# Exchanging the places of two groups of tensors in SBUF: a stage-tensor region and the weight rings

## Fill

filler text here. filler text here. filler text here. filler text here. filler text here. filler text here. filler text here. filler text here. filler text here. filler text here. filler text here. filler text here. filler text here. filler text here. filler text here. filler text here. filler text here. filler text here. filler text here. filler text here. filler text here. filler text here. filler text here. filler text here. filler text here. filler text here. filler text here. filler text here. filler text here. filler text here. filler text here. filler text here. filler text here. filler text here. filler text here. filler text here. filler text here. filler text here. filler text here. filler text here. filler text here. filler text here. filler text here. filler text here. filler text here. filler text here. filler text here. filler text here. filler text here. filler text here. filler text here. filler text here. filler text here. filler text here. filler text here. filler text here. filler text here. filler text here. filler text here. filler text here. filler text here. filler text here. filler text here. filler text here. filler text here. filler text here. filler text here. filler text here. filler text here. filler text here. filler text here. filler text here. filler text here. filler text here. filler text here. filler text here. filler text here. filler text here. filler text here. filler text here. filler text here. filler text here. filler text here. filler text here. filler text here. filler text here. filler text here. filler text here. filler text here. filler text here. filler text here. filler text here. filler text here. filler text here. filler text here. filler text here. filler text here. filler text here. filler text here. filler text here. filler text here. filler text here. filler text here. filler text here. filler text here. filler text here. filler text here. filler text here. filler text here. filler text here. filler text here. filler text here. filler text here. filler text here. filler text here. filler text here. filler text here. filler text here. filler text here. filler text here. filler text here. filler text here. filler text here. filler text here. filler text here. filler text here. filler text here. filler text here. filler text here. filler text here. filler text here. filler text here. filler text here. filler text here. filler text here. filler text here. filler text here. filler text here. filler text here. filler text here. filler text here. filler text here. filler text here. filler text here. filler text here. filler text here. filler text here. filler text here. filler text here. filler text here. filler text here. filler text here. filler text here. filler text here. filler text here. filler text here. filler text here. filler text here. filler text here. filler text here. filler text here. filler text here. filler text here. filler text here. filler text here. filler text here. filler text here. filler text here. filler text here. filler text here. filler text here. filler text here. filler text here. filler text here. filler text here. filler text here. filler text here. filler text here. filler text here. filler text here. filler text here. filler text here. filler text here. filler text here. filler text here. filler text here. filler text here. filler text here. filler text here. filler text here. filler text here. filler text here. filler text here. filler text here. filler text here. filler text here. filler text here. filler text here. filler text here. filler text here. filler text here. filler text here. filler text here. filler text here. filler text here. filler text here. filler text here. filler text here. filler text here. filler text here. filler text here. filler text here. filler text here. filler text here. filler text here. filler text here. filler text here. filler text here. filler text here. filler text here. filler text here. filler text here. filler text here. filler text here. filler text here. filler text here. filler text here. filler text here. filler text here. filler text here. filler text here. filler text here. filler text here. filler text here. filler text here. filler text here. filler text here. filler text here. filler text here. filler text here. filler text here. filler text here. filler text here. filler text here. filler text here. filler text here. filler text here. filler text here. filler text here. filler text here. filler text here. filler text here. filler text here. filler text here. filler text here. filler text here. filler text here. filler text here. filler text here. filler text here. filler text here. filler text here. filler text here. filler text here. filler text here. filler text here. filler text here. filler text here. filler text here. filler text here. filler text here. filler text here. filler text here. filler text here. filler text here. filler text here. filler text here. filler text here. filler text here. filler text here. filler text here. filler text here. filler text here. filler text here. filler text here. filler text here. filler text here. filler text here. filler text here. filler text here. filler text here. filler text here. filler text here. filler text here. filler text here. filler text here. filler text here. filler text here. filler text here. filler text here. filler text here. filler text here. filler text here. filler text here. filler text here. filler text here. filler text here. filler text here. filler text here. filler text here. filler text here. filler text here. filler text here. filler text here. filler text here. filler text here. filler text here. filler text here. filler text here. filler text here. filler text here. filler text here. filler text here. filler text here. filler text here. filler text here. filler text here. filler text here. filler text here. filler text here. filler text here. filler text here. filler text here. filler text here. filler text here. filler text here. filler text here. filler text here. filler text here. filler text here. filler text here. filler text here. filler text here. filler text here. filler text here. filler text here. filler text here. filler text here. filler text here. filler text here. filler text here. filler text here. filler text here. filler text here. filler text here. filler text here. filler text here. filler text here. filler text here. filler text here. filler text here. filler text here. filler text here. filler text here. filler text here. filler text here. filler text here. filler text here. filler text here. filler text here. filler text here. filler text here. filler text here. filler text here. filler text here. filler text here. filler text here. filler text here. filler text here. filler text here. filler text here. filler text here. filler text here. filler text here. filler text here. filler text here. filler text here. filler text here. filler text here. filler text here. filler text here. filler text here. filler text here. filler text here. filler text here. filler text here. filler text here. filler text here. filler text here. filler text here. filler text here. filler text here. filler text here. filler text here. filler text here. filler text here. filler text here. filler text here. filler text here. filler text here. filler text here. filler text here. filler text here. filler text here. filler text here. filler text here. filler text here. filler text here. filler text here. filler text here. filler text here. filler text here. filler text here. filler text here. filler text here. filler text here. filler text here. filler text here. filler text here. filler text here. filler text here. filler text here. filler text here. filler text here. filler text here. filler text here. filler text here. filler text here. filler text here. filler text here. filler text here. filler text here. filler text here. filler text here. filler text here. filler text here. filler text here. filler text here. filler text here. filler text here. filler text here. filler text here. filler text here. filler text here. filler text here. filler text here. filler text here. filler text here. filler text here. filler text here. filler text here. filler text here. filler text here. filler text here. filler text here. filler text here. filler text here. filler text here. filler text here. filler text here. filler text here. filler text here. filler text here. filler text here. filler text here. filler text here. filler text here. filler text here. filler text here. filler text here. filler text here. filler text here. filler text here. filler text here. filler text here. filler text here. filler text here. filler text here. filler text here. filler text here. filler text here. filler text here. filler text here. filler text here. filler text here. filler text here. filler text here. filler text here. filler text here. filler text here. filler text here. filler text here. filler text here. filler text here. filler text here. filler text here. filler text here. filler text here. filler text here. filler text here. filler text here. filler text here. filler text here. filler text here. filler text here. filler text here. filler text here. filler text here. filler text here. filler text here. filler text here. filler text here. filler text here. filler text here. filler text here. filler text here. filler text here. filler text here. filler text here. filler text here. filler text here. filler text here. filler text here. filler text here. filler text here. filler text here. filler text here. filler text here. filler text here. filler text here. filler text here. filler text here. filler text here. filler text here. filler text here. filler text here. filler text here. filler text here. filler text here. filler text here. filler text here. filler text here. filler text here. filler text here. filler text here. filler text here. filler text here. filler text here. filler text here. filler text here. filler text here. filler text here. filler text here. filler text here. filler text here. filler text here. filler text here. filler text here. filler text here. filler text here. filler text here. filler text here. filler text here. filler text here. filler text here. filler text here. filler text here. filler text here. filler text here. filler text here. filler text here. filler text here. filler text here. filler text here. filler text here. filler text here. filler text here. filler text here. filler text here. filler text here. filler text here. filler text here. filler text here. filler text here. filler text here. filler text here. filler text here. filler text here. filler text here. filler text here. filler text here. filler text here. filler text here. filler text here. filler text here. filler text here. filler text here. filler text here. filler text here. filler text here. filler text here. filler text here. filler text here. filler text here. filler text here. filler text here. filler text here. filler text here. filler text here. filler text here. filler text here. filler text here. filler text here. filler text here. filler text here. filler text here. filler text here. filler text here. filler text here. filler text here. filler text here. filler text here. filler text here. filler text here. filler text here. filler text here. filler text here. filler text here. filler text here. filler text here. filler text here. filler text here. filler text here. filler text here. filler text here. filler text here. filler text here. filler text here. filler text here. filler text here. filler text here. filler text here. filler text here. filler text here. filler text here. filler text here. filler text here. filler text here. filler text here. filler text here. filler text here. filler text here. filler text here. filler text here. filler text here. filler text here. filler text here. filler text here. filler text here. filler text here. filler text here. filler text here. filler text here. filler text here. filler text here. filler text here. filler text here. filler text here. filler text here. filler text here. filler text here. filler text here. filler text here. filler text here. filler text here. filler text here. filler text here. filler text here. filler text here. filler text here. filler text here. filler text here. filler text here. filler text here. filler text here. filler text here. filler text here. filler text here. filler text here. filler text here. filler text here. filler text here. filler text here. filler text here. filler text here. filler text here. filler text here. filler text here. filler text here. filler text here. filler text here. filler text here. filler text here. filler text here. filler text here. filler text here. filler text here. filler text here. filler text here. filler text here. filler text here. filler text here. filler text here. filler text here. filler text here. filler text here. filler text here. filler text here. filler text here. filler text here. filler text here. filler text here. filler text here. filler text here. filler text here. filler text here. filler text here. filler text here. filler text here. filler text here. filler text here. filler text here. filler text here. filler text here. filler text here. filler text here. filler text here. filler text here. filler text here. filler text here. filler text here. filler text here. filler text here. filler text here. filler text here. filler text here. filler text here. filler text here. filler text here. filler text here. filler text here. filler text here. filler text here. filler text here. filler text here. filler text here. filler text here. filler text here. filler text here. filler text here. filler text here. filler text here. filler text here. filler text here. filler text here. filler text here. filler text here. filler text here. filler text here. filler text here. filler text here. filler text here. filler text here. filler text here. filler text here. filler text here. filler text here. filler text here. filler text here. filler text here. filler text here. filler text here. filler text here. filler text here. filler text here. filler text here. filler text here. filler text here. filler text here. filler text here. filler text here. filler text here. filler text here. filler text here. filler text here. filler text here. filler text here. filler text here. filler text here. filler text here. filler text here. filler text here. filler text here. filler text here. filler text here. filler text here. filler text here. filler text here. filler text here. filler text here. filler text here. filler text here. filler text here. filler text here. filler text here. filler text here. filler text here. filler text here. filler text here. filler text here. filler text here. filler text here. filler text here. filler text here. filler text here. filler text here. filler text here. filler text here. filler text here. filler text here. filler text here. filler text here. filler text here. filler text here. filler text here. filler text here. filler text here. filler text here. filler text here. filler text here. filler text here. filler text here. filler text here. filler text here. filler text here. filler text here. filler text here. filler text here. filler text here. filler text here. filler text here. filler text here. filler text here. filler text here. filler text here. filler text here. filler text here. filler text here. filler text here. filler text here. filler text here. filler text here. filler text here. filler text here. filler text here. filler text here. filler text here. filler text here. filler text here. filler text here. filler text here. filler text here. filler text here. filler text here. filler text here. filler text here. filler text here. filler text here. filler text here. filler text here. filler text here. filler text here. filler text here. filler text here. filler text here. filler text here. filler text here. filler text here. filler text here. filler text here. filler text here. filler text here. filler text here. filler text here. filler text here. filler text here. filler text here. filler text here. filler text here. filler text here. filler text here. filler text here. filler text here. filler text here. filler text here. filler text here. filler text here. filler text here. filler text here. filler text here. filler text here. filler text here. filler text here. filler text here. filler text here. filler text here. filler text here. filler text here. filler text here. filler text here. filler text here. filler text here. filler text here. filler text here. filler text here. filler text here. filler text here. filler text here. filler text here. filler text here. filler text here. filler text here. filler text here. filler text here. filler text here. filler text here. filler text here. filler text here. filler text here. filler text here. filler text here. filler text here. filler text here. filler text here. filler text here. filler text here. filler text here. filler text here. filler text here. filler text here. filler text here. filler text here. filler text here. filler text here. filler text here. filler text here. filler text here. filler text here. filler text here. filler text here. filler text here. filler text here. filler text here. filler text here. filler text here. filler text here. filler text here. filler text here. filler text here. filler text here. filler text here. filler text here. filler text here. filler text here. filler text here. filler text here. filler text here. filler text here. filler text here. filler text here. filler text here. filler text here. filler text here. filler text here. filler text here. filler text here. filler text here. filler text here. filler text here. filler text here. filler text here. filler text here. filler text here. filler text here. filler text here. filler text here. filler text here. filler text here. filler text here. filler text here. filler text here. filler text here. filler text here. filler text here. filler text here. filler text here. filler text here. filler text here. filler text here. filler text here. filler text here. filler text here. filler text here. filler text here. filler text here. filler text here. filler text here. filler text here. filler text here. filler text here. filler text here. filler text here. filler text here. filler text here. filler text here. filler text here. filler text here. filler text here. filler text here. filler text here. filler text here. filler text here. filler text here. filler text here. filler text here. filler text here. filler text here. filler text here. filler text here. filler text here. filler text here. filler text here. filler text here. filler text here. filler text here. filler text here. filler text here. filler text here. filler text here. filler text here. filler text here. filler text here. filler text here. filler text here. filler text here. filler text here. filler text here. filler text here. filler text here. filler text here. filler text here. filler text here. filler text here. filler text here. filler text here. filler text here. filler text here. filler text here. filler text here. filler text here. filler text here. filler text here. filler text here. filler text here. filler text here. filler text here. filler text here. filler text here. filler text here. filler text here. filler text here. filler text here. filler text here. filler text here. filler text here. filler text here. filler text here. filler text here. filler text here. filler text here. filler text here. filler text here. filler text here. filler text here. filler text here. filler text here. filler text here. filler text here. filler text here. filler text here. filler text here. filler text here. filler text here. filler text here. filler text here. filler text here. filler text here. filler text here. filler text here. filler text here. filler text here. filler text here. filler text here. filler text here. filler text here. filler text here. filler text here. filler text here. filler text here. filler text here. filler text here. filler text here. filler text here. filler text here. filler text here. filler text here. filler text here. filler text here. filler text here. filler text here. filler text here. filler text here. filler text here. filler text here. filler text here. filler text here. filler text here. filler text here. filler text here. filler text here. filler text here. filler text here. filler text here. filler text here. filler text here. filler text here. filler text here. filler text here. filler text here. filler text here. filler text here. filler text here. filler text here. filler text here. filler text here. filler text here. filler text here. filler text here. filler text here. filler text here. filler text here. filler text here. filler text here. filler text here. filler text here. filler text here. filler text here. filler text here. filler text here. filler text here. filler text here. filler text here. filler text here. filler text here. filler text here. filler text here. filler text here. filler text here. filler text here. filler text here. filler text here. filler text here. filler text here. filler text here. filler text here. filler text here. filler text here. filler text here. filler text here. filler text here. filler text here. filler text here. filler text here. filler text here. filler text here. filler text here. filler text here. filler text here. filler text here. filler text here. filler text here. filler text here. filler text here. filler text here. filler text here. filler text here. filler text here. filler text here. filler text here. filler text here. filler text here. filler text here. filler text here. filler text here. filler text here. filler text here. filler text here. filler text here. filler text here. filler text here. filler text here. filler text here. filler text here. filler text here. filler text here. filler text here. filler text here. filler text here. filler text here. filler text here. filler text here. filler text here. filler text here. filler text here. filler text here. filler text here. filler text here. filler text here. filler text here. filler text here. filler text here. filler text here. filler text here. filler text here. filler text here. filler text here. filler text here. filler text here. filler text here. filler text here. filler text here. filler text here. filler text here. filler text here. filler text here. filler text here. filler text here. filler text here. filler text here. filler text here. filler text here. filler text here. filler text here. filler text here. filler text here. filler text here. filler text here. filler text here. filler text here. filler text here. filler text here. filler text here. filler text here. filler text here. filler text here. filler text here. filler text here. filler text here. filler text here. filler text here. filler text here. filler text here. filler text here. filler text here. filler text here. filler text here. filler text here. filler text here. filler text here. filler text here. filler text here. filler text here. filler text here. filler text here. filler text here. filler text here. filler text here. filler text here. filler text here. filler text here. filler text here. filler text here. filler text here. filler text here. filler text here. filler text here. filler text here. filler text here. filler text here. filler text here. filler text here. filler text here. filler text here. filler text here. filler text here. filler text here. filler text here. filler text here. filler text here. filler text here. filler text here. filler text here. filler text here. filler text here. filler text here. filler text here. filler text here. filler text here. filler text here. filler text here. filler text here. filler text here. filler text here. filler text here. filler text here. filler text here. filler text here. filler text here. filler text here. filler text here. filler text here. filler text here. filler text here. filler text here. filler text here. filler text here. filler text here. filler text here. filler text here. filler text here. filler text here. filler text here. filler text here. filler text here. filler text here. filler text here. filler text here. filler text here. filler text here. filler text here. filler text here. filler text here. filler text here. filler text here. filler text here. filler text here. filler text here. filler text here. filler text here. filler text here. filler text here. filler text here. filler text here. filler text here. filler text here. filler text here. filler text here. filler text here. filler text here. filler text here. filler text here. filler text here. filler text here. filler text here. filler text here. filler text here. filler text here. filler text here. filler text here. filler text here. filler text here. filler text here. filler text here. filler text here. filler text here. filler text here. filler text here. filler text here. filler text here. filler text here. filler text here. filler text here. filler text here. filler text here. filler text here. filler text here. filler text here. filler text here. filler text here. filler text here. filler text here. filler text here. filler text here. filler text here. filler text here. filler text here. filler text here. filler text here. filler text here. filler text here. filler text here. filler text here. filler text here. filler text here. filler text here. filler text here. filler text here. filler text here. filler text here. filler text here. filler text here. filler text here. filler text here. filler text here. filler text here. filler text here. filler text here. filler text here. filler text here. filler text here. filler text here. filler text here. filler text here. filler text here. filler text here. filler text here. filler text here. filler text here. filler text here. filler text here. filler text here. filler text here. filler text here. filler text here. filler text here. filler text here. filler text here. filler text here. filler text here. filler text here. filler text here. filler text here. filler text here. filler text here. filler text here. filler text here. filler text here. filler text here. filler text here. filler text here. filler text here. filler text here. filler text here. filler text here. filler text here. filler text here. filler text here. filler text here. filler text here. filler text here. filler text here. filler text here. filler text here. filler text here. filler text here. filler text here. filler text here. filler text here. filler text here. filler text here. 

## The chip, the cores and the metric

The kernel runs on one core of one Trainium2 chip. The metric is the device time of one execution in microseconds (us); a median over several executions is compared.

## What is computed

The reference chains two small transformer blocks, each with two layers, over 256 tokens of width 1024, in float32.

```python
def reference(x, c, ctx, c_ctx, w_ada, ..., w_gate_2, w_up_2, w_down_2):
    x = first_block(x, c, ctx, c_ctx, w_ada, ...)      # 2 layers
    return second_block(x, attn_norm_g_2, w_in_2, ...) # 2 layers
```

A layer of the first block takes a modulation from the condition vectors (`silu(cond) @ w_ada`, 1024 x 6144), normalizes and modulates the latent and the context stream (256 tokens each), multiplies by `w_in` (1024 x 1536), mixes by attention, a Fourier transform and a gated spatial product, multiplies by `w_out` (1024 x 1024), and runs a squared-ReLU MLP of width 4096. In its second layer the context stream ends early. A layer of the second block multiplies the 256 latent tokens by `w_in_2` (1024 x 3656), runs three kinds of attention, multiplies by `w_out_2`, and runs a gated MLP of width 2816.

## The kernel before

The float32 products with weights are made of three products of a reduced format (`float32r`): a weight slot `raw` is split into a high part `w_hi` (ScalarE, `split`, L1101) and a rest `w_lo = raw - w_hi` (VectorE, `split`, L1467), an activation likewise into a high part and a rest, and `three` (L2049) issues three matmuls into the same PSUM tile: high by high, high by low and low by high. Of a matmul's two operands, one is loaded into TensorE (the stationary one, 128 columns, shown as LDWEIGHTS), the other streams through it (the moving one, 256, 328 or 512 columns). Which is which depends on the stage:

| stage (time in the profile) | moving | stationary | columns |
|---|---|---|---|
| `rows1`, `down("out1")` of the first block (30 to 113, 200 to 247, 620 to 675, 720 to 750) | ring of weights | `act_hi`, `act_lo` | 512 |
| `up1`, first block's MLP in, layer 0 (247 to 345, 443 to 522) | `act_hi`, `act_lo` | ring of weights | 512 |
| `up1`, layer 1 (750 to 850) | `act_hi`, `act_lo` | ring of weights | 256 |
| `down("mlp1")`, MLP out (345 to 435, 522 to 607, 850 to 939) | ring of weights | `hid1_hi`, `hid1_lo` | 512 |
| `rows2`, `down("out2")` of the second block (940 to 1090, 1284 to 1433) | ring of weights | `act_hi`, `act_lo` | 512, 328, 256 |
| `up2` (1095 to 1221, 1437 to 1564) | `act_hi`, `act_lo` | ring of weights | 256 |
| `down("mlp2")` (1221 to 1283, 1564 to 1625) | ring of weights | `hid2_hi`, `hid2_lo` | 512 |

The rings are `raw` and `w_lo` with 8 slots and `w_hi` with 5, each slot 1024 floats (4,096 bytes) per partition. In the second block `w_hi` has a sixth slot, in a tensor of its own, `w_hi2` (`hi_of`): of each six consecutive slots of weights one has its high part there. In the profile's names buffer numbers are left out, so `w_hi2` reads `w_hi`, `hid1_hi` and `hid2_hi` read `hid_hi`. The slots are filled by DMAs from SyncE's queue in the fixed order of the program (`put`, L804); 40 slots of `w_lo` are stored to HBM and fetched back later (`split_lo`).

The modulation (`ada`, L2118) multiplies plain float32 out of `raw` by `cond` in 32-column tiles. Every wait is a semaphore; the order of the work on each engine is written out by hand in tables (`FILL`, `FILL2`, `OUT2`).

SBUF is laid out by hand as well. `sb` hands out tensors one behind the other in the order of the calls, each start rounded up to 32 bytes, and what is entered in an `ExitStack` gives its bytes back when the `with` ends, so that what is allocated next lies on the same bytes. So `raw` and `w_lo` share one place (`w_lo` overwrites a slot of `raw` as it is computed), and the tensors of the two blocks' stages share one region:

```python
        with ExitStack() as s:
            raw = sb("raw", [P, RAW, 1024], F32, s)
        w_lo = sb("w_lo", [P, RAW, 1024], F32R)
        w_hi = sb("w_hi", [P, SPLIT, 1024], F32R)
```

## Time and profile before

| | |
|---|---|
| median of 3 runs | 1634.4 us (1633.2 to 1635.25) |
| the profiled execution's own time | 1630.14 us |
| its span | 1628.3 us |
| granted TensorE clock, mean | 0.995 |
| TensorE matmuls (PE) | 1571.9 us busy, 97% of the span |
| weight loads (PEld) | 1280.5 us, 79% |
| VectorE (DVE) | 1029.1 us, 63% |
| ScalarE (ACT) | 793.5 us, 49% |
| GpSimd (POOL) | 115.2 us, 7% |
| moved by DMA | 322.41 MB, mean 198 GB/s |

Busy time is the time in which at least one instruction of the engine is in flight. Matmuls overlap each other, so their mean duration is longer than the distance from one start to the next; the distance (the pitch) is what a stream of matmuls costs. In the chain of waits a piece "PE ... x48" gives it: its time divided by its count.

### The profile page before, as it was taken

How to read it: one execution, taken by the hardware profiler on the slowest of the kernel's cores; microseconds unless marked ns; L12 is line 12 of the kernel's file. 1: busy time of each engine (PE TensorE's matmuls, PEld its weight loads, DVE VectorE, ACT ScalarE, POOL GpSimd, SP SyncE). 2: the span in 40 equal slices, each digit the busy share in tenths (PEclk: the TensorE clock that was granted, in tenths of full speed). 3: DMA queues.
4: the chain of work that ended last, by engine and by line, in shares of the span. 5: the costliest groups of instructions: out<-in, count | busy, mean ns of one | idle time of the engine just before them, and what ended most of it. 6: DMA issues, size and time to landing. Idle time of an engine off the chain costs nothing.

```text
span 1628.3 us, 23404 instructions
## 1 busy us (share of the span) xinstructions
PE 1571.9 (97%) x9126; PEld 1280.5 (79%) x9126; DVE 1029.1 (63%) x1585; ACT 793.5 (49%) x1346; POOL 115.2 (7%) x130
## 2 busy tenths in 40 slices
PE   6999999999999998998999999999999999999999
PEld 2864776788888887567998878779998787799987
DVE  3637654663356327576775476878885558878863
ACT  3536623551246225564664456655454456555442
POOL 0211000000000001100000030100000101000000
PEclk8999999999999999999999999999999999999999
DMA  9438533882367433576998699336665696356653
GB/s 358 143 115 295 199 97 123 279 282 93 108 232 275 149 91 100 186 263 193 336 322 269 195 302 307 119 117 182 184 188 185 197 318 205 96 146 187 186 183 114
DMA packets 201005, 322.41 MB, mean 198 GB/s; under 512 B 14576, under 2 KB 100864, under 8 KB 200768
## 3 DMA queue, kind: packets, MB, share of 16 engines
q1 hardware_dynamic: 192992, 293.51, 56.0%
q0 software_dynamic: 7680, 27.34, 4.6%
q8 instruction: 73, 1.20, 0.3%
q14 instruction: 36, 0.29, 0.1%
q10 hardware_dynamic: 224, 0.07, 0.0%
HBM read 298.27 MB, written 22.61 MB: 197 GB/s over the span
## 4 chain that ended last, share of the span: by engine, by line
PE 89%; DVE 5%; DMA 3%; ACT 2%; issue 1%; POOL 1%; SPq 0%; POOLq 0%; DVEq 0%; ACTq 0%
PE bank L2049 54%; PE pair_bank L2049 21%; PE bank L2118 2%; PE pair_bank L2309 1%; PE bank L2340 1%; PE bank L2320 1%; PE pair_bank L2360 1%; PE bank L2582 1%; PE bank L2250 1%; DVE w_lo L1467 1%; DMA raw<-in_w_in 1%; PE bank L2144 1%; DMA raw<-in_w_ada 1%; PE bank L2230 1%; DMA raw<-in_w_mlp 1%
## 5 line engine op out<-in xcount | busy, mean ns | idle before, releaser
L1467 DVE TENSOR_TENSOR w_lo<-raw,w_hi 128x1024 fp32r<-128x1024 f32 (+1 forms) x374 | 447.9, 1219 | 283.7 <-ACT w_hi L1101 281.8
L1101 ACT CAST w_hi<-raw 128x1024 fp32r<-128x1024 f32 (+2 forms) x416 | 427.7, 1044 | 389.6 <-PE bank L2049 285.8
L2049 PE MATMUL pair_bank<-act_hi,w_hi 128*128 128x256 f32 (+1 forms) x736 | 230.4, 313 | 8.7 <-DVE act_lo L1545 3.4
L2049 PE MATMUL pair_bank<-act_hi,w_lo 128*128 128x256 f32 (+1 forms) x736 | 227.0, 308 | 0.0
L2049 PE MATMUL pair_bank<-act_lo,w_hi 128*128 128x256 f32 (+1 forms) x736 | 226.9, 308 | 0.0
L2049 PE MATMUL bank<-w_hi,hid_lo 128*128 128x512 f32 x560 | 221.3, 395 | 0.0
L2049 PE MATMUL bank<-w_hi,hid_hi 128*128 128x512 f32 x560 | 221.3, 395 | 0.0
L2049 PE MATMUL bank<-w_lo,hid_hi 128*128 128x512 f32 x560 | 221.3, 395 | 0.0
L2049 PE MATMUL bank<-w_hi,act_hi 128*128 128x512 f32 (+2 forms) x528 | 205.9, 390 | 6.5 <-DVE act_lo L1578 2.1
L2049 PE MATMUL bank<-w_hi,act_lo 128*128 128x512 f32 (+2 forms) x528 | 199.2, 377 | 0.0
L2049 PE MATMUL bank<-w_lo,act_hi 128*128 128x512 f32 (+2 forms) x528 | 198.9, 377 | 0.0
L2049 PEld LDWEIGHTS pair_bank<-act_hi,w_hi 128*128 128x128 f32 x736 | 140.2, 190 | 23.5 <-DVE act_lo L1545 5.7
L2049 PEld LDWEIGHTS pair_bank<-act_lo,w_hi 128*128 128x128 f32 x736 | 140.2, 191 | 7.4 <-issue 1.0
L2049 PEld LDWEIGHTS pair_bank<-act_hi,w_lo 128*128 128x128 f32 x736 | 140.2, 191 | 6.9
L2049 PE MATMUL bank<-act_hi,w_hi 128*128 128x256 f32 (+1 forms) x480 | 145.0, 302 | 0.6 <-DVE w_lo L1467 0.6
L2049 PE MATMUL bank<-act_hi,w_lo 128*128 128x256 f32 (+1 forms) x480 | 144.3, 301 | 0.0
L2049 PE MATMUL bank<-act_lo,w_hi 128*128 128x256 f32 (+1 forms) x480 | 144.3, 301 | 0.0
L2049 PEld LDWEIGHTS bank<-w_hi,hid_lo 128*128 128x128 f32 x560 | 105.1, 188 | 25.5
L2049 PEld LDWEIGHTS bank<-w_lo,hid_hi 128*128 128x128 f32 x560 | 105.1, 188 | 25.3
L2049 PEld LDWEIGHTS bank<-w_hi,hid_hi 128*128 128x128 f32 x560 | 105.2, 188 | 25.2
L2049 PEld LDWEIGHTS bank<-w_hi,act_hi 128*128 128x128 f32 x528 | 99.7, 189 | 27.7 <-issue 4.2
L2049 PEld LDWEIGHTS bank<-w_hi,act_lo 128*128 128x128 f32 x528 | 99.5, 188 | 18.7
(238 smaller groups left out, 2102.3 us busy)
## 6 DMA issues: line engine op xcount, KB each, us to landing
raw<-in_w_mlp SPq DMA_DIRECT2D x128, 512.0 KB, 4.4
raw<-in_w_in SPq DMA_DIRECT2D x112, 512.0 KB, 4.5
raw<-in_w_ada SPq DMA_DIRECT2D x96, 512.0 KB, 5.7
raw<-in_w_gate SPq DMA_DIRECT2D x44, 512.0 KB, 3.8
raw<-in_w_up SPq DMA_DIRECT2D x44, 512.0 KB, 3.8
raw<-in_w_down SPq DMA_DIRECT2D x44, 512.0 KB, 3.5
split_lo<-w_lo POOLq DMA_DIRECT2D x36, 512.0 KB, 4.9
w_lo<-split_lo SPq DMA_DIRECT2D x36, 512.0 KB, 5.1
```

The lines of the kernel that those rows point to most:

```text
L1101: nc.scalar.copy(hi_of(i)[:, 0:w], raw[:, i % RAW, 0:w]).then_inc(hi_ready, 1)
L1467: nc.vector.tensor_tensor(w_lo[:, i % RAW, 0:w], raw[:, i % RAW, 0:w], hi_of(i)[:, 0:w].bitcast(F32), ALU.subtract).then_inc(lo_ready, 1)
L2049: ins = nc.tensor.matmul(o, a[x], b[y], start=first and i == 0, stop=True, skip_group_check=True)
L2118: ins = nc.tensor.matmul(bank[bk][j:j + 32, :], cond[:, k, :], tiles(raw[:, r, :], 2)[:, kk, :], start=k < 4, stop=True, skip_group_check= ...
L2144: nc.tensor.matmul(bank[bk][:], sel_b[:, s, :], mod_rows[:, bk % 2, :], start=True, stop=True, skip_group_check=True).then_inc(ada_turned, 1)
L2230: ins = nc.tensor.transpose(bank[b][:, i * P:(i + 1) * P], x, ident)
L2250: ins = nc.tensor.matmul(bank[5][:], proj1[:, 2 * s + t, F1 + i * P:F1 + (i + 1) * P], dft_n[:, t, :], start=t == 0, stop=t == TT - 1)
L2309: nc.tensor.matmul(bank[a][:, 0:w], st["q"][a], st["k"][a], start=True, stop=True).then_inc(scored, 1)
L2320: ins = nc.tensor.matmul(st["o"][a], st["v"][a][kt], probs_t1[:, j % 2, a, kt, :], start=kt == 0, stop=kt == keys - 1)
L2340: ins = nc.tensor.transpose(bank[2 + a][:, kt * P:(kt + 1) * P], probs1[:, j % 2, a, kt * P:(kt + 1) * P], ident)
L2360: nc.tensor.matmul(bank[a][:, 0:w], st["q"][a], st["k"][a], start=True, stop=False)
L2582: ins = nc.tensor.matmul(bank[2][:, (h - h0) * wd:(h - h0 + 1) * wd], pair("iq", h, t * P, t * P + P), pairs_t[half:half + DH, PAIR["ik"], ...
```

## Rows read from the trace of the kernel before

**Rows 1.** The page: busy us (share) and count; busy tenths and granted clock.
```profile
PE 1571.9 (97%) x9126; PEld 1280.5 (79%) x9126; DVE 1029.1 (63%) x1585; ACT 793.5 (49%) x1346; POOL 115.2 (7%) x130
...
PE   6999999999999998998999999999999999999999
...
PEclk8999999999999999999999999999999999999999
```

**Rows 2.** Chain of waits: shares of the span.
```profile
PE 89%; DVE 5%; DMA 3%; ACT 2%; issue 1%; POOL 1%; SPq 0%; POOLq 0%; DVEq 0%; ACTq 0%
```

**Rows 3.** Costliest groups by shape: count, busy us, mean ns, idle before.
```profile
L1467 DVE TENSOR_TENSOR w_lo<-raw,w_hi 128x1024 fp32r<-128x1024 f32 x368 | 441.7, 1222 | 276.5 <-ACT w_hi L1101 274.6
L1101 ACT CAST w_hi<-raw 128x1024 fp32r<-128x1024 f32 x404 | 417.0, 1047 | 369.4 <-PE bank L2049 283.3 <-PE pair_bank L2049 62.7 <-DMA raw<-in_w_mlp 13.3
L2049 PE MATMUL bank<-w_hi,hid_lo 128*128 128x512 f32 x560 | 221.3, 395 | 0.0
...
L2049 PE MATMUL bank<-w_hi,act_hi 128*128 128x512 f32 x448 | 181.0, 404 | 5.7 <-DVE act_lo L1578 2.1 <-DVE w_lo L1467 1.9 <-DMA w_lo<-split_lo 1.2
...
L2049 PE MATMUL pair_bank<-act_hi,w_hi 128*128 128x256 f32 x560 | 160.1, 286 | 6.8 <-DVE act_lo L1545 2.5 <-DVE w_lo L1467 2.1 <-DVE act_lo L1578 2.1
...
L2049 PE MATMUL bank<-act_hi,w_lo 128*128 128x256 f32 x400 | 113.2, 283 | 0.0
...
L2049 PE MATMUL pair_bank<-act_hi,w_hi 128*128 128x512 f32 x176 | 70.3, 399 | 2.0 <-DVE act_lo L1545 0.8 <-DVE w_lo L1467 0.6 <-ACT fa L1372 0.5
...
L2118 PE MATMUL bank<-raw,cond 128*32 128x512 f32 x384 | 51.8, 623 | 6.2 <-DMA raw<-in_w_ada 5.2 <-DVE cond L1477 1.1
```

**Rows 4.** Chain of waits, first 60 us: start us, us, what.
```profile
4.52 11.47 DMA raw<-in_w_ada
...
45.60 14.54 PE bank L2049 x64
```

**Rows 5.** Chain of waits, whole span, its longest pieces.
```profile
345.20 89.59 PE bank L2049 x384
...
500.07 10.88 PE pair_bank L2049 x48
...
826.64 11.52 PE pair_bank L2049 x96
...
951.35 8.75 DMA w_lo<-split_lo
...
1118.12 11.47 PE pair_bank L2049 x96
...
1221.48 61.47 PE bank L2049 x264
...
1300.20 7.98 DMA raw<-in_w_in
```

**Rows 6.** Single matmuls of rows2 in order: start us, us, engine, line.
```profile
973.74 0.39 PE L2049 MATMUL bank<-w_hi,act_hi 128*128 128x512 f32 x1
...
975.10 0.39 PE L2049 MATMUL bank<-w_hi,act_hi 128*128 128x512 f32 x1
...
977.67 0.40 PE L2049 MATMUL bank<-w_hi,act_lo 128*128 128x512 f32 x1
```

**Rows 7.** The same, single matmuls of up2.
```profile
1141.17 0.28 PE L2049 MATMUL pair_bank<-act_hi,w_lo 128*128 128x256 f32 x1
...
1143.77 0.28 PE L2049 MATMUL pair_bank<-act_hi,w_hi 128*128 128x256 f32 x1
...
1145.93 0.28 PE L2049 MATMUL pair_bank<-act_hi,w_hi 128*128 128x256 f32 x1
```

**Rows 8.** Busy us of each engine by stretch; granted clock, DMA share, GB/s.
```profile
10.00:40.00 30.00, 20.86 (x106) 10.29 (x103) 12.17 (x37) 13.81 (x34) 1.98 (x2) 0.83 1.03 384
...
939.00:1095.00 156.00, 147.85 (x829) 115.76 (x828) 115.49 (x269) 91.47 (x211) 27.07 (x24) 1.00 0.65 214
1095.00:1221.00 126.00, 126.00 (x1054) 126.00 (x1055) 109.05 (x88) 62.55 (x77) 0.00 (x0) 1.00 0.62 181
```

56 lines of the change are left out of this document (29 added, 27 removed).

## Prediction

> **What bounds the kernel now.** I read the page first, then the chain of waits, then the groups by shape, and then single matmuls. TensorE is busy for 97% of the span, nine tenths or more in 37 of the 40 slices, at full clock behind the first slice [rows 1]. The chain that ended last runs through it for 89% of the span; VectorE has 5% of it, DMA 3%, ScalarE 2% [rows 2]. So the price of this change is, above all, what it does to the pitch of TensorE's matmuls, and, next, to the waits for transfers. The instructions are the same before and after; what differs is the byte at which each operand lies.
>
> The trace shows that such a thing can matter. Four stages run long stretches without any idle time, so their pitch can be read from the chain [rows 5]. Where both operands are rings or `act` tensors, 48 matmuls of 512 columns take 10.88 us, 226.7 ns each; the same with the roles exchanged gives 14.54 us for 64, 227.2 ns [rows 4]. Where the stationary operand is `hid1`, 384 matmuls of the same shape take 89.59 us, 233.3 ns, 6.6 ns more. With `hid2` it is 61.47 us for 264, 232.8 ns. The duration column does not show this well (395 ns against 404, since it has waits in it) [rows 3]; the pitch does. With 256 columns and both operands in rings and `act`, 96 take 11.52 us, 120.0 ns. None of these stretches waits for anything, so the difference lies in the operands, and all that differs is where they lie. By the table of starts, rings and `act` tensors start at a multiple of 128 bytes; `hid1` starts 32 bytes behind one and `hid2` 96 bytes behind one.
>
> A third case is in the trace: `w_hi2`, which starts 64 bytes behind a multiple of 128. As the moving operand in `rows2` it has 11 pitches from 975.10 to 977.67 us, 233.6 ns each, right behind six of an ordinary ring slot from 973.74 to 975.10, 226.7 ns [rows 6]. As the stationary operand in `up2` it goes the other way: 22 pitches from 1141.17 to 1143.77 us, 118.2 ns, then 18 of the next slot to 1145.93, 120.0 ns [rows 7].
>
> **The change part by part.** The plain reading of these rows is that the pitch hangs on the remainder of the starts within 128 bytes. I take it as the rule for the sum and price each tensor by it.
>
> 1. Rings, `const`, `act`. All keep remainder 0. Price 0: 226.7 and 120.0 ns stay. This is the term with the greatest weight, since 3 x 448 and 3 x 176 matmuls of 512 columns and 3 x (560 + 400) of 256 columns hang on it [rows 3]. The nearest rows bound it: upwards 6.6 ns more per 512-column matmul (as `hid1`), which is 1,872 x 6.6 ns = 12.4 us; downwards 1.8 ns less per 256-column matmul (as `w_hi2`), about 2,530 x 1.8 ns = 4.6 us when the sixth that `w_hi2` has already is left out. I take 0, since among the starts seen those with remainder 0 agree wherever in their tensors they lie.
>
> 2. `hid1` goes from remainder 32 to 96, `hid2` from 96 to 32. Both remainders are in the trace, at 233.3 and 232.8 ns, and the second has one slot in six with `w_hi2` in it. Exchanging them costs 0; the lost `w_hi2` mixture costs 0.5 ns x 2 x 264 = +0.3 us. Full relief of both would be 3 x 560 x 6.6 ns = -11.1 us [rows 3], and it needs a remainder 0, which they don't get.
>
> 3. `w_hi2` goes from remainder 64 to 0. In `up2` its slots lose their advantage. The two stretches have 1,054 and as many matmuls [rows 8], a sixth of them is 350, by 1.8 ns = +0.6 us; the chain's pieces of 96 say about the same, 11.47 us here against 11.52 in `up1`, which has no `w_hi2` [rows 5]. In `rows2` and `down("out2")` it gains: 12 slots by the ring's count, 12 matmuls each, by 6.9 ns = -1.0 us. But these slots are where TensorE waits between slots (147.85 us busy in 156) [rows 8], so part of it only lengthens a wait. I take half, -0.5 us, with 0 and -1.0 as ends.
>
> 4. `cond` goes from remainder 0 to 64 as the stationary operand of the modulation (L2118, 384 rows for 192 matmuls, 623 ns) [rows 3]. With 7 ns either way it is 1.3 us at most. I take 0, because much of that work stands in the first 40 us behind its transfers [rows 4].
>
> 5. VectorE and ScalarE. The split takes 1222 ns and the cast 1047 ns for 1024 elements [rows 3]; both work on the rings, whose remainder by 128 stays. I take 0. If it were 1% on both, the cover is their idle time (276.5 and 369.4 us ahead of these two groups), save in the starts of stages where the chain goes through them.
>
> 6. Transfers. Nothing changes in number, size, order or queue. I take 0; the bound is in the rivals.
>
> Sum: +0.3 + 0.6 - 0.5 = +0.4 us. The profiled execution took 1630.14 us, so it would be 1630.5; the median of the runs is 1634.4, 4.3 us above it, and the forecast on that scale is 1634.8 us. A measurement of this kernel can tell about 0.2%, 3.3 us, from no change, so this is no change.
>
> The Trainium skill ("SBUF — State Buffer", specifications and the section on the bandwidth-pool intuition) says that lines of SBUF are 16 bytes and that TensorE has two read ports of its own, independent for moving and stationary operands. By that, starts at multiples of 32 bytes would all cost the same and the sum would be 0.0. The trace does not agree: 233.3 against 226.7 ns.
>
> **The rivals.**
>
> *Slower: the offset between rings and `act` counts beyond 128 bytes.* Before, rings and `act` tensors all start at 128 by the remainder of 256; now the rings start at 0 and `act` stays at 128. No steady stretch before has two operands that differ by just 128, so the trace cannot exclude that this costs what 32 bytes cost in `hid1`. It decides in the stages `rows1`, `down("out1")`, `up1`, `rows2`: if it hits both roles, +12.4 us, 1647.2; if only the rings as stationary operand (528 matmuls), +3.5 us, 1638.3. For it: a difference of 64 in `w_hi2` did change the pitch, by +6.9 ns when moving. Against: nothing in the trace varies with a larger remainder.
>
> *Faster: the same offset helps.* As with `w_hi2` in `up2`, the 256-column matmuls fall from 120.0 to 118.2 ns: -4.6 us, and the +0.6 of step 3 is not lost: 1629.6.
>
> *Faster: it is not the remainder but the half of SBUF.* `hid1`, `hid2` and `w_hi2` all lie above byte 131,072 before, the rings and `act` below it. If `hid` is slow for that reason, it now gets 226.7 ns for most of its parts: -11.1 us, 1623.7, and 1627.2 if the rings as stationary operand pay the same price in 528 matmuls. For it: the `w_hi2` rows fit neither reading well. Against: there `w_hi2` above the line is faster, not slower, with 256 columns.
>
> *Faster by transfers.* From 10 to 40 us the DMA engines are busy throughout (share 1.03, 384 GB/s) [rows 8] and the chain waits 11.47 us for them [rows 4]; later waits are 8.75 and 7.98 us [rows 5]. If a packet into `raw` gets cheaper by 128 of its 2,048 bytes, 6% of 30 us is -1.9 us, 1632.9, which is within no change. The Trainium skill ("DMA: Bandwidth & Descriptors", how a descriptor splits into AXI transactions) says that a transaction must start at a multiple of 256 bytes and that what lies before an unaligned start is fetched for nothing. The slots of `raw` start at remainder 128 before and 0 now, and by that rule this is the case that comes true. No row here shows it.
>
> That the change does not do what it says can be put aside: the starts in the built program are the new ones, and `hole` adds no instruction.
>
> **How the numbers follow.** Forecast 0.56, transfers 0.05, faster by the offset 0.12, faster by the half 0.08, slower in one role 0.07, slower in both 0.12. Within 0.2% are the first two, 0.61; faster 0.20; slower 0.19. The range takes in the forecast, the transfers, the gain by the offset and the loss in one role; left out are the loss in both roles and the half of SBUF, 0.20. With the ends of steps 3 and 4 it is 1628 to 1640 us.
>
> **What the profile after would show.** Right: 226.7 ns for 512 columns in `up1` (10.88 us for 48), 233.3 ns with `hid1` and `hid2` (89.6 us for 384, 61.6 for 264), 120.0 ns for every piece of `up2` (11.52, no 11.47), 226.7 ns for the sixth slot in `rows2`. Wrong: a pitch other than 226.7 or 120.0 ns in any of the long stretches with rings and `act` (the offset), 226.7 ns in the stretch from 345 us (the half), or a first chain piece for `raw<-in_w_ada` shorter than 11 us with the clock and matmuls unchanged (the transfers).

## The result, and the change that it belongs to

The part ahead of the prediction went on record with a mistake of mine: right behind the title it holds a block of filler words that says nothing, and its section on the change is missing, with the table of starts that the prediction reads. That section stands here instead. It is not part of what was recorded; its table follows from the calls of `sb` in the two kernels.

### The change

The calls of `sb` are put in another order. Before: `residual`, `act_hi`, `act_lo`, then `raw`/`w_lo`, `w_hi`, `const` and the small tensors, then the stages' tensors. Now the stages' tensors come directly behind `act_lo`; a tensor `hole` of 24,352 floats (97,408 bytes) per partition, which nothing reads or writes, is allocated when they have been given back, so that it covers just their region; and `raw`/`w_lo`, `w_hi`, `const` and the small tensors lie behind it.

```diff
+HOLE = 24352
...
         act_lo = sb("act_lo", [P, KT, 2 * NT], F32R)
-        with ExitStack() as s:
-            raw = sb("raw", [P, RAW, 1024], F32, s)
-        w_lo = sb("w_lo", [P, RAW, 1024], F32R)
-        w_hi = sb("w_hi", [P, SPLIT, 1024], F32R)
-        const = sb("const", [P, sum(CONSTS.values())])
...
-        lam = sb("lam", [P, DEPTH, 8])
-        g_rows = residual
-
         with ExitStack() as s:
             cond_raw = sb("cond_raw", [P, KT, 2], F32, s)
...
             with ExitStack() as s2:
                 xn2 = sb("xn2", [P, TT, D], F32, s2)
+        hole = sb("hole", [P, HOLE])
+        with ExitStack() as s:
+            raw = sb("raw", [P, RAW, 1024], F32, s)
+        w_lo = sb("w_lo", [P, RAW, 1024], F32R)
+        w_hi = sb("w_hi", [P, SPLIT, 1024], F32R)
+        const = sb("const", [P, sum(CONSTS.values())])
...
+        lam = sb("lam", [P, DEPTH, 8])
+        g_rows = residual
```

No instruction is added, removed, moved or given another shape: the diff touches calls of `sb` alone, and the two traces have the same count of instructions on every engine. Only the bytes differ at which operands lie. These are the starts in bytes within a partition, with the remainder by 128 and by 256:

| tensor | before | mod 128 | mod 256 | after | mod 128 | mod 256 |
|---|---|---|---|---|---|---|
| `residual` | 16512 | 0 | 128 | 16512 | 0 | 128 |
| `act_hi` | 32896 | 0 | 128 | 32896 | 0 | 128 |
| `act_lo` | 49280 | 0 | 128 | 49280 | 0 | 128 |
| `raw`, `w_lo` | 65664 | 0 | 128 | 163072 | 0 | 0 |
| `w_hi` | 98432 | 0 | 128 | 195840 | 0 | 0 |
| `const` | 118912 | 0 | 128 | 216320 | 0 | 0 |
| `cond` | 131712 | 0 | 128 | 65728 | 64 | 192 |
| `w_hi2` | 134720 | 64 | 64 | 68736 | 0 | 128 |
| `hid1_hi` | 155296 | 32 | 160 | 89312 | 96 | 224 |
| `hid1_lo` | 188064 | 32 | 160 | 122080 | 96 | 224 |
| `hid2_hi` | 138848 | 96 | 96 | 72864 | 32 | 160 |
| `hid2_lo` | 161376 | 96 | 96 | 95392 | 32 | 160 |
| `proj1` | 155296 | 32 | 160 | 89312 | 96 | 224 |

All stage tensors move down by 65,984 bytes, the rings and constants up by 97,408 bytes. Parts of a tensor begin at multiples of 512 bytes from its start in the large products, save the 328-column slots of `rows2`, which begin at multiples of 1,312 bytes.

### The times

| | before | after |
|---|---|---|
| median of 5 runs | 1634.4 us (1633.2 to 1635.25) | 1642.83 us (1636.96 to 1644.41) |
| the profiled execution | 1630.14 us, span 1628.3 | 1643.58 us, span 1641.8 |
| granted TensorE clock, mean | 0.995 | 0.988 |

The ratio is 1.0041, with an interval of 1.0029 to 1.0052. By the medians the kernel is slower by 8.4 us, by the ratio by 6.7 us (4.7 to 8.5). The forecast was no change, 1634.8, and the time lies outside the range of 1628 to 1640. The median of before is over five runs here; the part ahead had three of them, with the same median.

The page of the kernel after: busy us and counts, the granted clock in 40 slices, and the shares of the chain (beside [rows 1, 2]).

```profile
PE 1588.1 (97%) x9126; PEld 1285.7 (78%) x9126; DVE 1029.3 (63%) x1585; ACT 793.8 (48%) x1346; POOL 115.2 (7%) x130
...
PEclk8999999999999999999999999999999999999999
...
PE 90%; DVE 4%; DMA 2%; ACT 2%; issue 1%; POOL 1%; SPq 0%; POOLq 0%; DVEq 0%; ACTq 0%
```

TensorE is busy 16.2 us longer with the same 9,126 matmuls, and the chain's shares are those of before to within a point. So it is the pitch, not a new wait. The groups by shape (count, busy us, mean ns, idle before), beside [rows 3]:

```profile
L1469 DVE TENSOR_TENSOR w_lo<-raw,w_hi 128x1024 fp32r<-128x1024 f32 x368 | 441.5, 1221 | 279.8 <-ACT w_hi L1103 278.2
L1103 ACT CAST w_hi<-raw 128x1024 fp32r<-128x1024 f32 x404 | 416.9, 1047 | 371.3 <-PE bank L2051 281.2 <-PE pair_bank L2051 68.2 <-DMA raw<-in_w_mlp 14.2
L2051 PE MATMUL bank<-w_hi,hid_lo 128*128 128x512 f32 x560 | 221.4, 395 | 0.0
...
L2051 PE MATMUL bank<-w_hi,act_hi 128*128 128x512 f32 x448 | 182.6, 408 | 4.3 <-DVE act_lo L1580 2.1 <-DVE w_lo L1469 1.9 <-DMA w_lo<-split_lo 0.3
...
L2051 PE MATMUL bank<-act_hi,w_lo 128*128 128x256 f32 x400 | 112.5, 281 | 0.0
...
L2051 PE MATMUL pair_bank<-act_hi,w_hi 128*128 128x512 f32 x176 | 71.2, 404 | 1.6 <-DVE act_lo L1547 0.6 <-DVE w_lo L1469 0.6 <-ACT fa L1374 0.2
...
L2051 PE MATMUL bank<-act_hi,w_hi 128*128 128x512 f32 x80 | 32.5, 406 | 0.6 <-DVE w_lo L1469 0.6
```

VectorE and ScalarE keep their means to 0.3%. With `hid` nothing moved; with `act` and 512 columns the mean went up (404 to 408, 399 to 404 ns), with 256 it went down (283 to 281). The pitch shows it better. The chain of waits, its longest pieces (start us, us, what), beside [rows 4, 5]:

```profile
4.78 11.54 DMA raw<-in_w_ada
...
45.92 30.67 PE bank L2051 x132
77.47 22.39 PE bank L2051 x96
...
351.11 89.60 PE bank L2051 x384
...
507.90 11.20 PE pair_bank L2051 x48
...
823.37 11.39 PE pair_bank L2051 x96
...
965.03 8.08 DMA w_lo<-split_lo
...
1132.85 11.39 PE pair_bank L2051 x96
...
1235.41 61.65 PE bank L2051 x264
```

| piece | before | after | pitch before, after |
|---|---|---|---|
| moving ring, stationary `act`, 512 columns, x132 | 29.95 | 30.67 | 226.9, 232.3 ns |
| moving `act`, stationary ring, 512 columns, x48 | 10.88 | 11.20 | 226.7, 233.3 ns |
| stationary `hid1`, 512 columns, x384 | 89.59 | 89.60 | 233.3, 233.3 ns |
| moving `act`, stationary ring, 256 columns, x96 | 11.52 | 11.39 | 120.0, 118.6 ns |
| stationary `hid2`, x264 | 61.47 | 61.65 | 232.8, 233.5 ns |

Over all uninterrupted stretches the mean pitch of the 512-column group is 232.4 to 232.9 ns in both roles, so 5.7 to 6.2 ns more than before. The groups by shape have 3 x (448 + 176 + 80) = 2,112 such matmuls. The sum: 144 of them lie in slots that have their high part in `w_hi2` and lose nothing (their mean pitch, from the starts of the single matmuls in the second block, was 233.7 ns before and is 232.2 after, -0.2 us), the other 1,968 x 5.7 ns are +11.2 us. In each `up2` the ten pieces from 1106.65 to 1221.48 us took 114.83 us before and take 113.96 now (1121.45 to 1235.41), -0.9 us each; the 772 matmuls of 256 columns in `up1` give -1.0 us. That is +8.2 us, an estimate: with 6.2 ns in place of 5.7 it would be 9.2. Beside it stand 8.4 us by the medians and 6.7 by the ratio, so the pitches account for the loss, to within about 2 us. The profiled execution lost 13.5 us in its span. The rest goes with its clock, as the windows show (stretch, length, busy us of PE, PEld, DVE, ACT, POOL, then granted clock, DMA share, GB/s):

```profile
200.00:260.00 60.00, 57.18 (x267) 46.23 (x266) 30.26 (x59) 19.64 (x45) 3.23 (x5) 0.97 0.27 84
535.00:640.00 105.00, 101.24 (x466) 82.45 (x465) 44.09 (x66) 30.66 (x52) 3.68 (x5) 0.98 0.34 108
640.00:760.00 120.00, 113.87 (x684) 78.39 (x682) 77.15 (x158) 67.99 (x132) 11.87 (x10) 0.97 0.60 195
760.00:860.00 100.00, 96.28 (x777) 91.27 (x778) 71.50 (x79) 62.82 (x80) 6.41 (x12) 0.98 0.86 295
```

All four stood at a granted clock of 1.00 before (2.4 GHz); the missing 2 and 3% make 9.5 us at most. Why the clock was lower there, no run shows. The change's loss doesn't hang on this: another run of it had a clock of 0.996 and a span of 1635.2 us, still 6.9 above before's 1628.3 at 0.995.

### The profile page after: what moved, and what is told of

Same layout as the page of the kernel before. It is cut to its first block, busy times and chain, and to the rows that moved or that the text cites. A ratio compares the mean times of both kernels' runs of the same rounds, so it can differ in the third digit from the quotient of the medians.

```text
span 1641.8 us, 23404 instructions
## 1 busy us (share of the span) xinstructions
PE 1588.1 (97%) x9126; PEld 1285.7 (78%) x9126; DVE 1029.3 (63%) x1585; ACT 793.8 (48%) x1346; POOL 115.2 (7%) x130
## 4 chain that ended last, share of the span: by engine, by line
PE 90%; DVE 4%; DMA 2%; ACT 2%; issue 1%; POOL 1%; SPq 0%; POOLq 0%; DVEq 0%; ACTq 0%
PE bank L2051 55%; PE pair_bank L2051 21%; PE bank L2120 2%; PE pair_bank L2311 1%; PE bank L2342 1%; PE bank L2322 1%; PE pair_bank L2362 1%; PE bank L2252 1%; PE bank L2584 1%; DVE w_lo L1469 1%; DMA raw<-in_w_ada 1%; PE bank L2146 1%; PE bank L2232 1%; DMA raw<-in_w_mlp 1%; POOL xrstd L976 1%
```

## The experiments

Every kernel here computes all of the reference; the edits are paddings, that is, calls of `sb` for tensors that nothing uses, so the instructions stay those of before. Unless said otherwise they start from the kernel before, whose rings and `act` both start at 128 by the remainder of 256. "Offset" is the start of the stationary operand less that of the moving one, by the remainder of 256. Ratios are to the kernel before in the same comparison.

### Which part of the move costs: offset, height or place

`e1_low_128`: rings stay low, but 128 bytes off `act`.

```diff
         act_lo = sb("act_lo", [P, KT, 2 * NT], F32R)
+        pad = sb("pad", [P, 32])
```

> The layout of before with 128 bytes of padding behind act_lo, so that the rings start 128 bytes further on by the remainder of 256, as in the changed kernel, but stay low in SBUF. Theory A (the offset between rings and act by the remainder of 256 or more sets the pitch): 512 columns with rings and act at 232 to 234 ns, 256 columns at 118.7 ns, MLP out with hid1 unchanged at 233.3 ns, total about +7 us (1641). Theory B (the height in SBUF sets it, rings above byte 131,072 against act below): 226.7 and 120.0 ns, total 1634.4.

1638.43 us, ratio 1.0031 (1.0018 to 1.0044). Its chain of waits:

```profile
324.97 11.15 PE pair_bank L2050 x48
347.27 89.59 PE bank L2050 x384
...
803.91 11.39 PE pair_bank L2050 x96
```

11.15 us for 48 (232.3 ns) and 11.39 for 96 (118.6 ns): both pitches of the kernel after, without its exchange of places. `hid1` and its ring are 32 bytes apart as before, and keep their 89.59 us.

`e2_high_0`: the changed kernel with `stat` and `xvar` allocated ahead of the rings, which moves the rings by 384 bytes more, so that they are high but at offset 0.

```diff
         hole = sb("hole", [P, HOLE])
+        stat = sb("stat", [P, 8, 2 * TT, 2])
+        xvar = sb("xvar", [P, 8, 2 * TT])
         with ExitStack() as s:
             raw = sb("raw", [P, RAW, 1024], F32, s)
```

> The changed layout with stat and xvar moved ahead of the rings, which so start 384 bytes higher and have the same remainder by 512 as act, 128, but lie high in SBUF. Theory A (offset): 226.7 ns for 512 columns and 120.0 ns for 256 come back, total near 1634 to 1635. Theory B (height): 232 to 234 and 118.7 ns stay, total as changed, 1640 to 1644.

1635.98 us, ratio 1.0004 (0.9995 to 1.0013). The loss is gone with the places exchanged all the same. Its chain:

```profile
325.15 10.88 PE pair_bank L2051 x48
346.91 89.96 PE bank L2051 x384
...
813.81 11.52 PE pair_bank L2051 x96
...
1569.42 61.61 PE bank L2051 x264
```

10.88 and 11.52 are before's. The stretch with `hid1`, whose offset here is 96, has 234.3 ns, 1.0 more than at 32 or 224. `e3_both_128` puts the same pad of 32 floats ahead of `residual`, so that rings and `act` both move by 128 and stay aligned; `e4_low_256` makes the pad of `e1_low_128` 64 floats, an offset of 256.

> The layout of before with 128 bytes of padding ahead of residual, so that act and rings all move by 128 and start at remainder 0 by 256. Theory A as a difference between the two operands: nothing moves, 226.7 and 120.0 ns, 1634.4. Theory A2 (each operand's own remainder by 256 counts, for the moving or the stationary one): pitches change, to 232 to 234 ns for 512 columns, total up by 5 us or more. Theory B: nothing moves.

> The layout of before with 256 bytes of padding behind act_lo: the offset between rings and act is 256 by the remainder of 512, 0 by the remainder of 256. If the period is 256 or less: 226.7 and 120.0 ns, 1634.4. If it is 512 or more: other pitches, between 224 and 234 ns for 512 columns. Theory B: nothing moves.

1632.92 us, ratio 0.9987 (0.9976 to 0.9998), and 1634.44 us, ratio 1.0000 (0.9990 to 1.0011). Both chains have 10.88 us for 48 matmuls and 89.59 for 384, as before. So neither the height nor the absolute start counts, only the offset, and it repeats after 256 bytes. The loss of the change is shown to be the offset of 128 that it puts between rings and `act`.

### What the offset of `hid` costs

`e5_hid_0`: `w_hi2`, `hid1` and `hid2` are padded to the rings' remainder, offset 0 everywhere.

```diff
             with ExitStack() as s2:
+                pad_h1 = sb("pad_h1", [P, 120], F32, s2)
...
+            pad_w2 = sb("pad_w2", [P, 16], F32, s)
             w_hi2 = sb("w_hi2", [P, SPLIT2 - SPLIT, 1024], F32R, s)
...
             with ExitStack() as s2:
+                pad_h2 = sb("pad_h2", [P, 120], F32, s2)
```

> The layout of before with padding ahead of w_hi2, hid1_hi and hid2_hi alone, so that all of them start at the same remainder by 256 as the rings and act. Theory A (the offset between the two operands by the remainder of 256, best at 0 for 512 columns): MLP out with hid1 and hid2 falls from 233.3 and 233.1 ns to 226.7 ns, 1,680 matmuls by 6.6 ns = -11.1 us, total 1623.3, MLP out of layer 0 from 89.6 to 87.0 us for 384. w_hi2 in up2 goes up to 120.0 ns, +0.9 us. Rival (hid lies high in SBUF or is slow for its own contents): 233.3 ns stays, total 1634.4 to 1635.

1621.95 us, ratio 0.9913 (0.9900 to 0.9927), 12.8 us faster by the medians (by the ratio 11.9 to 16.3). Its chain:

```profile
345.74 87.04 PE bank L2052 x384
...
811.60 11.52 PE pair_bank L2052 x96
...
1560.82 59.88 PE bank L2052 x264
```

87.04 us for 384 is 226.7 ns, 59.88 for 264 is 226.8. The 11.1 us that step 2 of the prediction put on full relief of `hid` were there to be had by a padding of under 500 bytes in each place. `e8_hid_map` tries two other offsets, with 24 floats in place of 120 and no `pad_w2` (`hid1` at offset 128, `hid2` at 64):

> The layout of before with hid1 128 bytes and hid2 64 bytes off the rings by the remainder of 256 (24 floats of padding ahead of each). Theory A: hid1 as rings and act in the changed kernel, 232.4 ns, 1.0 us less over 1,152 matmuls; hid2 at 64 as w_hi2 did, 230 to 234 ns. Total 1632 to 1635. Rival (period 128 for hid): hid1 at 226.7 ns, total 1627.

1634.6 us, ratio 1.0001 (0.9991 to 1.0011): 89.24 us for 384, 232.4 ns, and 61.47 for 264, 232.8. No relief.

### The map of offsets

Four more paddings of the place of `e1_low_128`: 16, 8, 24 and 48 floats (in `e10_low_96`, `w_hi2`, `hid1` and `hid2` are padded as well: to offsets 0, 192 and 224 from the rings; its expectation below has 160 for the last, a slip).

> The layout of before with 64 bytes of padding behind act_lo: rings and act 64 apart. Theory A by the row of w_hi2 before: 256 columns with rings as stationary operand fall to 116 to 118 ns (-5 to -10 us over 2,880), 512 columns rise to 232 to 234 ns (+11 us over 1,870). Total 1634 to 1641. Rival (only 0 against 128 matters, w_hi2 was odd for the alternation with w_lo): 226.7 and 120.0 ns stay, 1634.4.

> The layout of before with 32 bytes of padding behind act_lo. Theory A: 512 columns with rings and act at 233.3 ns as with hid1, +12 us; hid1 stays 32 from the rings and at 233.3; for 256 columns no row shows 32 bytes, between 116 and 127 ns. Total 1640 to 1655. Rival (32 bytes hurt hid1 because of the stationary operand's own start, not the difference): stages with act as stationary operand stay at 226.7 ns.

> A map of further offsets: the layout of before with 96 bytes behind act_lo, and hid1 and hid2 placed 192 and 160 bytes ahead of the rings by the remainder of 256. Theory A: every offset that is not 0 gives 228 to 234 ns for 512 columns and less than 120.0 ns for 256. A rival (multiples of 64 and odd multiples of 32 are the only two kinds): 96 and 160 as 32, 233.3 ns.

> The layout of before with 192 bytes behind act_lo. Theory A with a sign (the stationary operand 64 ahead is not the same as 64 behind): with act stationary, 64 ahead of the rings, 233.3 ns as for the rings 64 ahead of act in e6_low_64; with the rings stationary, 64 behind act, 229 ns. Without a sign: the same as e6_low_64, 233.3 and 229 in the same stages. 256 columns: 113.3 ns without a sign, another value with one.

`e6_low_64` gave 1632.65 us, 0.9988 (0.9978 to 0.9997); `e7_low_32` 1642.25, 1.0043 (1.0028 to 1.0058); `e10_low_96` 1637.85, 1.0016 (1.0002 to 1.0030); `e11_low_192` 1636.44, 1.0012 (0.9997 to 1.0027). The chain of `e6_low_64`:

```profile
76.27 21.97 PE bank L2050 x96
...
326.80 11.20 PE pair_bank L2050 x48
...
817.50 10.88 PE pair_bank L2050 x96
...
1135.12 11.31 PE bank L2050 x96
```

That of `e7_low_32`:

```profile
78.01 22.40 PE bank L2050 x96
...
330.15 11.20 PE pair_bank L2050 x48
...
807.22 11.36 PE pair_bank L2050 x96
```

That of `e10_low_96`:

```profile
78.15 22.40 PE bank L2053 x96
...
328.63 11.24 PE pair_bank L2053 x48
351.12 87.91 PE bank L2053 x384
...
803.18 11.39 PE pair_bank L2053 x96
...
1126.79 11.26 PE pair_bank L2053 x96
...
1469.11 11.39 PE pair_bank L2053 x96
```

And that of `e11_low_192`:

```profile
77.84 22.40 PE bank L2050 x96
...
329.01 10.99 PE pair_bank L2050 x48
...
820.30 11.31 PE pair_bank L2050 x96
```

By piece over count, from the pieces above and the others of the same chains (with 256 columns, `up1` first, then `up2` where it differs):

| offset | 512 columns, ns | 256 columns, ns |
|---|---|---|
| 0 | 226.7 to 227.2 | 120.0 |
| 32 | 233.3 to 233.4 | 118.3 |
| 64 | 232.8 to 233.3 | 113.3 or 117.8 |
| 96 | 234.2 to 234.3 | 118.6; 117.3 in one `up2` |
| 128 | 232.3 to 233.3 | 118.6 |
| 160 | 233.3 to 233.5 | |
| 192 | 228.9 | 117.8; 117.2 to 118.3 in `up2` |
| 224 | 232.8 to 233.4 | |

The stretches of `hid2`, the ends 232.8, 233.4 and 233.5, have one slot in six with `w_hi2`, which can lie at another offset, so they are less clean than the rest.

The sign counts: 21.97 us for 96 in `e6_low_64`, 10.99 for 48 in `e11_low_192` and 87.91 for 384 in `e10_low_96` are all an offset of 192, 228.9 ns, with `act` as the stationary operand in the first, a ring in the second and `hid1` in the third, while 64 gives 233.3. With 512 columns offset 0 is the best, with 256 columns the worst. That is why one padding moves the two kinds of stage in opposite directions and the sum over the kernel is small.

### A version that uses both

`e9_two_views`: the alignments of `e5_hid_0`, and `act_hi` and `act_lo` in one tensor with 16 spare floats, so that from the MLP of layer 1 of the first block on, the same data lie 64 bytes lower. Then the stages that stream `act` have offset 0 with 512 columns and offset 64 with 256. The stages of the second block with `act` stationary pay for it, with an offset of 192.

```diff
+        both = sb("act", [P, 2 * KT * 2 * NT + 16], F32R)
...
+                self.views = [tiles(both[:, at + part * full:at + (part + 1) * full], KT) for at in (16, 0)]
...
                 ph.down("out1", l, 1, KT, tiles_of(l), m + 1)
+                now[0] = l
```

> The layout of before with w_hi2, hid1 and hid2 lined up with the rings (as in e5_hid_0), and act_hi and act_lo in one tensor with 64 bytes to spare: up to the attention output of layer 1 of the first block they are used at the rings' remainder by 256, from the MLP of that layer on 64 bytes lower, so that the rings as stationary operand lie 64 bytes ahead of the moving act in all stages with 256 columns. Theory A: up1 of layer 1 and up2 fall from 120.0 to 113.3 ns, 2,880 matmuls by 6.7 ns = -19.3 us against e5_hid_0; 512 columns with act as stationary operand in the second block go from 227 to 229 ns, +1.5 us. Total near 1604, if ScalarE and VectorE keep up in up2 (VectorE was busy 109 of 126 us). Rival (they don't keep up): up2 pieces of 96 stay over 11.2 us and the waits for w_lo grow, total 1612 to 1618.

1611.69 us, ratio 0.9861 (0.9839 to 0.9883). Its chain:

```profile
345.47 87.04 PE bank L2064 x384
...
804.23 10.88 PE pair_bank L2064 x96
...
1108.77 11.31 PE pair_bank L2064 x96
...
1445.69 10.88 PE pair_bank L2064 x96
...
1543.61 59.87 PE bank L2064 x264
```

`up1` of layer 1 and `up2` of layer 1 have 10.88 us for 96, 113.3 ns. `up2` of layer 0 has 11.31, 117.8 ns, with the same tensors at the same starts, so 11 pieces x 0.43 = 4.7 us of the expected gain are missing. That is most of the 7.7 us by which the run missed the expected 1604; the other 3.0 are less than the 7.1 us between its fastest and its slowest execution. Two causes of the slower layer can be put aside. One piece of each layer, in the order of the windows above (stretch, length, busy us of PE, PEld, DVE, ACT, POOL, then granted clock, DMA share, GB/s):

```profile
1097.47:1108.77 11.30, 11.30 (x98) 11.30 (x98) 9.97 (x9) 5.76 (x7) 0.00 (x0) 1.00 0.67 186
1434.81:1445.69 10.88, 10.88 (x98) 10.88 (x98) 9.97 (x8) 5.76 (x7) 0.00 (x0) 1.00 0.67 195
```

The granted clock is 1.00 in both. And TensorE waits for nobody between 1097 and 1210 us, so the expectation's rival, that ScalarE and VectorE don't keep up, is not the cause, though the total of 1612 that it gave came out. `e12_two_views_128` moves all of it by 128 bytes (32 floats ahead of `residual`).

> e9_two_views with every tensor moved up by 128 bytes (32 floats of padding ahead of residual), so that all offsets between operands are those of e9. Theory A (offsets alone): total as e9, 1611.7 within 3 us. In e9 up2 ran at 117.8 ns in layer 0 and at 113.3 ns in layer 1 with the same offsets. If that is a matter of the instructions and offsets, the same two values come again in the same layers (11.31 and 10.88 us per 96). If it is a matter of how a stretch begins in time, either layer may show either value. If absolute starts matter, other values than these two come up.

1608.98 us, ratio 0.9844 (0.9827 to 0.9861), not to be told from `e9_two_views`. Its chain:

```profile
825.33 10.88 PE pair_bank L2065 x96
...
1113.60 11.31 PE pair_bank L2065 x96
...
1450.64 10.88 PE pair_bank L2065 x96
```

The same layer has the 11.31 again, and the other the 10.88. So the two values are not chance from run to run, and not the absolute place; in `e6_low_64`, where `w_hi2` isn't aligned with the rings, both layers have 11.31, beside 10.88 in `up1`. Nor is it only offset 64: `e10_low_96` has 11.26 in layer 0 and 11.39 in layer 1 (117.3 and 118.6 ns), the other way round. Within a layer of `e9_two_views` slots of all places in the rings have the same mean, 117.8 or 113.3 ns, so it isn't the place of a slot either. What sets the two values stays open: I had expected offset alone to decide.

## Why the prediction was wrong

**Reading and rule.** That TensorE's pitch decides, that it is read from uninterrupted pieces of the chain, and that `hid1` and `hid2` pay 6.6 ns per matmul for where they lie was right: `e5_hid_0` shows the last. The rule drawn from it was wrong. The prediction said that the pitch hangs on the remainder of the starts by 128 bytes, taken tensor by tensor. It is the offset between the two operands, by 256 bytes: `e3_both_128` moves both and changes nothing, `e1_low_128` moves one by 128 and costs 1.0031. The rows before held only offsets of 0, 32 and 224 (and those of `w_hi2`), and both rules fit them. The rows of `w_hi2`, which the prediction called a third case, fall into place by the offset: as the moving operand it was at 64, 233.6 ns there and 233.3 in the table, and as the stationary one at 192, 118.2 and 117.8.

**Step 1** failed, the term with the greatest weight: it priced rings and `act` at 0 because both keep remainder 0 by 128, and by the pitches it was +11.2 us for 512 columns and about -3 us for 256. Both bounds, +12.4 and -4.6, came true together in kind, since the slower rival and the faster one by the same offset are one mechanism with two signs by the number of columns. I gave them 0.12 each as if one excluded the other; their sum, +7.8, would have been 1642.6 us, beside 1642.83 measured. The count was too small as well: 1,872 left out the 3 x 80 matmuls of 512 columns in a second group with `act` moving.

**Step 2** (+0.3) was right, with 89.59 to 89.60 and 61.47 to 61.65 us, +0.4 us for both stretches of `hid2`; but not because remainders were exchanged. The offsets went from 32 to 224 for `hid1` and from 224 to 160 for `hid2`, and all three cost about the same; that was luck. **Step 3**: the +0.6 in `up2` is in the stretches' sum of -0.9 us each and had the right sign for `w_hi2` itself (its mean pitch went from 116.3 to 119.2 ns; 120.0 was forecast); of the gain in `rows2` and `down("out2")` little came, 233.7 to 232.2 ns in the slots with `w_hi2`, where 226.7 was forecast. `w_hi2` is aligned with `act` there now, but the `w_lo` of the same slot, which alternates with it, lies in the ring, 128 off. In `e2_high_0`, where both are aligned, these slots have 228.3 ns and the ordinary ones of the same stages 228.8, so there they pay nothing more. **Steps 4 and 5** held: 623 to 624 ns for the modulation, 1222 to 1221 ns for the split and 1047 in both for the cast.

**Step 6 and the transfers.** The first wait is 11.54 us where it was 11.47, and 10 to 40 us moved 383 GB/s where it was 384. `raw` starts at remainder 0 now, so the rule of the Trainium skill ("DMA: Bandwidth & Descriptors", on AXI transactions) on unaligned starts would have had its gain here; the wait does not show one. The page's sentence speaks of what a transaction reads, and `raw` is where these transfers write, so the prediction stretched it. Something else does differ: the main queue's packets took 54.0% of the span (page, DMA queues), 886.6 us of each engine, beside 56.0% of 1628.3, 911.8 us.

```profile
q1 hardware_dynamic: 192992, 293.51, 54.0%
```

In `e1_low_128` and `e3_both_128`, where `raw` starts at remainder 0 too, it is 55.7% of 1637.0 and 55.9% of 1627.9, 911.8 and 910.0 us, and 915.2 in `e2_high_0`. So neither the remainder nor the height gives it alone; it isn't settled, and no time hangs on it that the chain shows.

**The halves of SBUF** are excluded: `hid1_hi`, wholly below byte 131,072 now, keeps its 89.60 us, and `e2_high_0` has the high rings without loss. The Trainium skill ("SBUF — State Buffer", on the bandwidth-pool intuition) has TensorE read moving and stationary operands through ports of their own. No run here tests the ports, but the pitch depends on how the two starts stand to each other: 226.7, 228.9, 232.4, 233.3 or 234.2 ns for the same matmul. So the prediction's sum of 0.0 from that page does not hold here. Why the offset counts was not tested and stays open.

## What to carry to other kernels

Where TensorE bounds a kernel, compare the pitch of equal matmuls in uninterrupted stretches; where it differs by tensor, lay out moving and stationary operands so that their starts agree by the remainder of 256 bytes for 512 columns, and try other offsets for 256 columns, each stage for itself. All of this was measured on `float32r` matmuls of 128 stationary columns alone. Measure such a rule by moving one operand, then both: remainders that agree in a trace can hide a difference. And two rivals with one cause are not alternatives, their prices are added.

## What I had not expected

- The offset's effect reverses with the width: from 0 to 128 bytes it costs 512 columns 5.7 ns (2.5%) and gives 256 columns 1.4 ns (1.2%).
- At offset 64 the 256-column matmul has a pitch of 113.3 ns in two stages and 117.8 in another with the same layout, in both versions with two views.
- Layout alone took the kernel from 1633.45 to 1608.98 us, ratio 0.9844, with every instruction but its addresses the same.
